# Output projection of a hybrid layer in another order: convolution's part of both token blocks first, then the attention's part

## What is computed

```python
def reference(x, norm_mix_g, w_in, b_f, b_glu, w_dw, b_dw, ln_g, ln_b, w_out,
              norm_ffn_g, w_router, b_router, w_gu, b_gu, w_down, b_down, norm_final_g):
    h = x                                    # (1, 256, 1024)
    xn = rmsnorm(h, norm_mix_g)
    proj = xn @ w_in                         # q, k, v, forget gates, glu_in
    ...
    att_o = forgetting_attention(heads(q), heads(k), heads(v), log_f)   # 8 heads of 64
    conv_o = conformer_conv(glu_in, w_dw, b_dw, ln_g, ln_b)             # width 31, 512 channels
    mixed = jnp.concatenate([att_o, conv_o], axis=-1)
    h = h + mixed @ w_out
    hn = rmsnorm(h, norm_ffn_g).reshape(B * T, D)
    h = h + moe_ffn(hn, w_router, b_router, w_gu, b_gu, w_down, b_down).reshape(B, T, D)
    return rmsnorm(h, norm_final_g)
```

## Time and profile before

| | us |
|---|---|
| median of 3 runs | 1098.61 |
| lowest and highest run | 1097.21, 1099.31 |
| the profiled execution | 1100.79 |
| its span (first to last instruction) | 1098.8 |
| PE busy in the span | 1050.4 |
| DVE, ACT, POOL busy in the span | 239.3, 130.2, 43.6 |
| HBM read in the span | 421.13 MB |

### The profile page before, as it was taken

One profiled execution on the slowest core, in us unless ns is written; L12 is line 12 of the kernel. 1 busy time (PEld: TensorE's weight loads), 2 busy tenths in 40 slices (PEclk: granted clock), 3 DMA queues, 4 the chain that ended last, 5 costly groups with the idle time before them and its releaser, 6 DMA issues.

```text
span 1098.8 us, 14433 instructions
## 1 busy us (share of the span) xinstructions
PE 1050.4 (96%) x5846; PEld 431.8 (39%) x5847; DVE 239.3 (22%) x533; ACT 130.2 (12%) x245; POOL 43.6 (4%) x37
## 2 busy tenths in 40 slices
PE   9988999999999999999999999999999999999996
PEld 7864543333333333333333333333333333333332
DVE  3997341111111111101111111111111111111112
ACT  3224221000000000000000000000000000000002
POOL 7015010000000000000000000000000000000000
PEclk9998999999999999999999999999999999999999
DMA  9966089999999999999999999999999999999993
GB/s 298 384 282 261 11 310 396 419 418 417 416 415 417 416 417 416 418 417 418 417 417 417 417 415 416 417 416 418 418 417 418 416 416 416 417 416 417 417 417 130
DMA packets 84370, 423.27 MB, mean 385 GB/s; under 512 B 8917, under 2 KB 13065, under 8 KB 51528
## 3 DMA queue, kind: packets, MB, share of 16 engines
q1 hardware_dynamic: 81832, 421.37, 94.6%
q10 hardware_dynamic: 2464, 0.85, 0.3%
HBM read 421.13 MB, written 1.05 MB: 384 GB/s over the span
## 4 chain that ended last, share of the span: by engine, by line
PE 94%; DVE 2%; ACT 2%; issue 1%; DMA 1%; SPq 0%; DVEq 0%
PE work L972 76%; PE resid L972 14%; ACT region_x L632 2%; PE work L1269 2%; PE work L1283 1%; DMA ring<-in_w_dw 1%; DVE amax L757 0%; PE work L1077 0%; DVE region_m L785 0%; PE work L1159 0%; DVE top_i L849 0%; PE work L987 0%; SPq L307 0%; DVE region_q L965 0%; DVE spare L783 0%
## 5 line engine op out<-in xcount | busy, mean ns | idle before, releaser
L972 PE MATMUL work<-ring,region_x 128*64 128x512 f32 (+1 forms) x2960 | 678.2, 600 | 22.6 <-ACT region_x L632 22.3
L972 PEld LDWEIGHTS work<-ring,region_x 128*64 128x64 f32 (+1 forms) x2960 | 207.8, 138 | 428.9 <-issue 401.9
L900 DVE TENSOR_SCALAR region_q<-work 128x512 f32<-128x512 f32 x32 | 22.1, 691 | 784.1 <-PE work L972 784.1
L972 PE MATMUL resid<-region_x 128*128 128x512 f32 x256 | 126.0, 615 | 0.9 <-DVE region_x L956 0.9
L630 ACT ACTIVATE region_q<-region_q 128x512 f32<-128x512 f32 x32 | 20.2, 630 | 556.2 <-DVE region_q L900 556.2
L972 PEld LDWEIGHTS resid<-region_x 128*128 128x128 f32 x256 | 43.6, 190 | 59.9 <-issue 59.9
L972 PEld LDWEIGHTS work<-select,region_m 128*128 128x128 bf16 x1584 | 48.0, 98 | 26.6 <-issue 26.6
L972 PE MATMUL work<-region_x,ring 128*128 128x256 f32 x256 | 55.5, 379 | 0.0
L972 PE MATMUL work<-select,region_m 128*128 128x64 bf16 x1584 | 51.9, 193 | 0.0
L972 PEld LDWEIGHTS work<-region_x,ring 128*128 128x128 f32 x256 | 48.6, 190 | 7.0 <-issue 0.4
L734 DVE SCALAR_TENSOR_TENSOR region_m<-region_m,dw_cols 128x256 f32<-128x256 f32 x116 | 46.5, 478 | 1.3 <-ACT region_m L509 1.2
(11 more groups left out here) (187 smaller groups left out, 369.9 us busy)
## 6 DMA issues: line engine op xcount, KB each, us to landing
ring<-in_w_gu SPq DMA_DIRECT2D x242, 1024.0 KB, 20.0
ring<-in_w_down SPq DMA_DIRECT2D x124, 1024.0 KB, 23.1
region_k<-in_w_gu SPq DMA_DIRECT2D x14, 1024.0 KB, 20.3
ring<-in_w_in SPq DMA_DIRECT2D x3, 2048.0 KB, 14.1
ring<-in_w_in SPq DMA_DIRECT2D x4, 1024.0 KB, 12.1
ring<-in_w_out SPq DMA_DIRECT2D x2, 2048.0 KB, 18.8
region_k<-in_w_down SPq DMA_DIRECT2D x4, 1024.0 KB, 23.2
region_q<-in_x SPq DMA_DIRECT2D x2, 512.0 KB, 4.0
```

The source lines that it names most:

```text
L900: V.tensor_scalar(gate_h, work[:, GATE_BANK, :], SWIGLU_LIMIT, None, ALU.min).then_inc(gate_clamped, 1)
L972: return nc.tensor.matmul(out_, lhsT, rhs, start=start, stop=stop, skip_group_check=True)
```

## The change

The list `fill` gets another order. All of the convolution's part is taken first, for both blocks, then the attention's part of block 0. And the transposes of h of block 0 (two calls of `turn_h`) are moved behind the first of the two attention projections of block 1.

```diff
@@ -1116,7 +1116,7 @@
             turn(1)
             scores(3)
             weigh_values(1)
-            fill = [("out_conv", 0, 1), ("out_att", 0, 0), ("out_att", 0, 1), ("out_conv", 1, 0), ("out_conv", 1, 1)]
+            fill = [("out_conv", 0, 1), ("out_conv", 1, 0), ("out_conv", 1, 1), ("out_att", 0, 0), ("out_att", 0, 1)]
             arrived("out_att")
 
             def fill_in(count_):
@@ -1175,11 +1175,11 @@
 
                 return mm(resid[:, t, h * HALF:(h + 1) * HALF], ident[:, :], x_again[:, t, h * HALF:(h + 1) * HALF], False, False)
 
-            turn_h(0, 0)
-            turn_h(0, 1)
             fill_in(1)
             pe.wait_ge(att_copied, 2)
             project("out_att", 1, 0).then_inc(h_done, 1)
+            turn_h(0, 0)
+            turn_h(0, 1)
             project("out_att", 1, 1).then_inc(h_done, 1)
             turn_h(1, 0)
             pe.wait_ge(router_in, 32)
```

## The result

The changed kernel takes 1103.6 us (median of 8 runs, 1102.49 to 1108.71) against 1099.1 us (8 runs, 1097.21 to 1101.22). The ratio is 1.0049 with a 95% interval of 1.0035 to 1.0064: slower by 5.4 us, 3.8 to 7.0. Two later comparisons of the same two kernels gave 1.0052 (1.0035 to 1.0069) and 1.0039 (1.0024 to 1.0053). So the loss is 4 to 6 us, within the predicted range and 1 to 3 us under the forecast of +7.0.

What follows compares the result with a forecast made beforehand. PE was taken as the bound, with weights there in time. The terms 4.7 (PE's gaps and shift) + 0.8 (POOL) + 1.5 (clock) gave +7.0 us on 1098.6, so 1105.6 us; range 1102.6 to 1108.2.

Steps and rivals of the forecast that it cites:

- The bound: Over the span, PE sets the end and weights arrive in time; a later first expert moves the end equally.
- Step 1: Last projection of block 0 (attention half 1) starts on PE at 131.25 and ends at 134.7 us, before at 126.1.
- the part at nothing: PE up to the last group's values: slots filled by projections of equal length, 3.49 us each, so no cost.
- Step 2: Before block 1's attention projection, PE waits 3.2 us for ACT's second copy of attention outputs, behind the square of block 0.
- the first gap: PE idle from 134.7 to 137.9 us, before the attention projection of block 1: 3.2 us.
- Step 3: Before block 1's transposes, PE waits about 1.3 us for DVE's sum L869; the shift there is 4.7 us.
- the second gap: PE idle about 1.3 us from 145.8 us, before the transpose of block 1, until DVE's sum L869.
- Step 4: POOL's third part of block 0 (L456) holds DVE's L681, making L684 0.8 us later; bounds 0 and 0.8.
- Step 5: After PE's 3.2 us gap the clock falls to the 1.2 GHz level, costing 1.5 us; bounds 0 and 3.0.
- rival (a): On PE the gaps open, but the clock stays full and perhaps POOL does not hold DVE: +4.7 to +5.5 us; chance 0.20.
- Step 6: Two 1 MB loads into the convolution's weight slots are issued 9.7 us sooner, at 126.1; gain for PE 0.

Runs made afterwards that it cites:

- The early copy: The changed kernel with ACT's second copy of attention outputs put ahead of its wait for h of block 0: ratio 1.0008 (1.0000 to 1.0017).

## Why the prediction was right, point by point

- **The bound.** PE sets the end; a delay of 4.3 us in front of the first expert with PE busy cost 4.9 us. The prediction said that weights are always there in time. That was too strong: in 8 of the 14 profiles the last expert waited 0.5 to 1.4 us for them (0.87 and 1.4 in two of the changed kernel's three). The window that I read it from, 1080 to 1085 us, lies behind the place of these waits (1067 to 1075 us) and could not show them.
- **Step 1 and the part at nothing.** Right. The places up to 130 us cost the same, and the projection of block 0 ended where it was put.
- **Step 2, the first gap.** Forecast 3.2 us, measured 3.15, with the releaser named. The early copy took it away.
- **Step 3, the second gap.** Forecast 1.3 us and a shift of 4.7; measured 1.17 and 4.85. The reading of it, PE's wait for L869, was only half of the cause: with its first half early the shift stayed at 1.20 of 1.44, because the squares on ACT stood behind L597 as well.
- **Step 4, POOL.** This term was wrong: forecast 0.8 us, measured 0. L681 started at 147.85, within POOL's L456 (147.07 to 149.20), and took 0.14 us. I took the value of an operation on 4 elements for one on a single element; the other bound, 0, was right. The Trainium skill (SBUF — State Buffer, "SBUF: two separate sides") says that among the engines only the port pair shared by VectorE and GpSimd causes contention, and that VectorE's own pair never waits. The held cast of 8 elements (2.00 us, 0.17 alone) agrees with it; the free operation on 1 element agrees only if it keeps to VectorE's own pair, which no run here shows by itself.
- **Step 5, the clock.** Forecast 1.5 us, measured 0 in the profiles and 0 to 1.6 in the totals. What failed is the step from one gap to another: a gap of 2.47 us had been followed by the slow level, so one of 3.2 should be. The gap of 2.47 us was followed by it in all 14 profiles, that of 3.15 us in none of four, the gaps of 1.03 and 0.36 us in one, and the loop's pause of 2.1 us three times of three in one profile and once of three in the next. The length of a gap alone does not decide it. The term should have been a chance times a price, and rival (a), +4.7 to +5.5 without the clock, is what came out.
- **Step 6, the transfers.** Right: two loads at 125.42, worth nothing.

The sum 4.7 + 0.8 + 1.5 was thus made of one term that was right to 0.2 us and two that were too large. The forecast was 1 to 3 us too high. The range held the result because it had been stretched down to take in rival (a), to which I had given a chance of 0.20; that the number fell inside it is no merit of the terms for POOL and the clock.

## What to carry to other kernels

When a list of filler work is put in another order, look at what the moved piece releases on the in-order engines, not at the pieces' own cost. Here a copy of 0.6 us that PE needed stood behind a square that waited for the moved projection, and the delay cost nothing as long as one projection covered it; of the second 3.15 us were paid, and another 1.4 us came from the transposes that were moved with it. Moving the copy made the same order nearly free (0.9 us, 0.0 to 1.9). And before a gap is closed, follow the chain past the instruction that ends it: closing the second gap only moved the wait to the next one.

## What the runs showed of the hardware

- A gap of 2.47 us on PE was followed by the 1.2 GHz level (granted clock 0.50) in all 14 profiles. One of 3.15 us was not in four profiles, while a pause of 1.96 to 2.25 us was, in 23 of 42 cases; each of these cost 1.1 to 1.7 us.
- A DVE cast on 8 elements was held for 2.00 us by a running operation of POOL, and took 0.17 us without it; a TENSOR_SCALAR on 1 element ran in 0.14 us in the middle of the same kind of POOL operation.
- With the queues moving 417 GB/s and PE busy 195 of 200 us, PE came to wait 0.5 to 1.4 us for weights in the last expert in 8 of 14 profiles: in all six in which only one of the three pauses was followed by the 1.2 GHz level, and in two of the eight with two or three. This fits a part of the time that PE loses to its clock being given back there, but the count of slow pauses alone does not decide it.
